# Spreading the k-tiles of the conditioning product over four column groups of TensorE

## The chip, the cores and the metric

The kernel runs on one core of a Trainium2 chip. The metric is the device time of one execution in microseconds, as the median over runs; smaller is better.

## The reference, cut to what matters

The reference chains two transformer blocks. The second one is modulated by a conditioning vector: for each of its two layers

```
adaln(cond, w, b) = silu(cond) @ w + b        # cond: 1024 values, w: 1024 x 6144
mod_lat = adaln(c,     mod_w[i], mod_b[i])
mod_ctx = adaln(c_ctx, mod_w[i], mod_b[i])
sh1, sc1, g1, sh2, sc2, g2 = split(mod, 6)    # shifts, scales and gates of the layer
```

Both conditioning vectors (`c` and `c_ctx`) go through the same weights, so this is a product of a 2 x 1024 matrix with a 1024 x 6144 matrix, once per layer of the second block. It depends on nothing that the first block computes. The first block has two layers; each has a delta-rule branch (a blockwise triangular inverse followed by a recurrence over four chunks of 64 tokens), a sparse attention branch, a memory branch and a feed-forward part.

## The kernel before, in words

All weights come as slabs of 128 x 1024 f32 (512 KB) through a ring of six slots that the DMA queue of SyncE fills in the order in which TensorE uses them. TensorE, VectorE and ScalarE each run one long hand-ordered program; they meet at semaphores. Seven of the eight PSUM banks are handed out in turn; the eighth, `mod_bank`, belongs to the modulation for the whole first block: its columns 256 to 511 take the running sum of one group of 256 modulation values as a row (one partition for each conditioning vector), its columns 0 to 191 collect the values once they are turned into columns (one value per partition).

The 6144 modulation columns of a layer are cut into 24 groups of 256 (`MOD_GROUPS`). A group needs two slabs, each with four k-tiles of 128 x 256, so eight k-tiles make the sum. Of the 24 groups of a layer, the first 12 (`MODS_ALONE`) are computed in full f32 between other products of the first block's layer with the same number, by `some_mods`, line L1705; the other 12 are computed with rounded operands beside the gate and branch weights, by `mixed_mod`, line L1693. The change is about the first 12 of each layer: 24 groups in all.

For each of these groups TensorE (a) turns the row of the group before with `turn_mods` (L1675: two transposes of a 2 x 128 piece; the groups of `mixed_mod` use L1677, two products of a 4 x 128 piece with `fold4`), having waited for `mods_row`, and (b) runs eight matmuls with `cond[:, j, :]` (128 x 2) as the stationary operand and the k-tile (128 x 256) as the moving one, all accumulating in partitions 0 and 1 of `mod_bank`. The profile shows each f32 matmul as two records, so eight k-tiles are 16 records. ScalarE then copies the row out (`mod_rows`, L2165) into `mrow`, which has two slots.

Where the 12 groups of a layer stand in TensorE's order:

- four in the stage that builds the decay matrices, one ahead of the `cum` product (L1768) of each quarter g of the heads; ScalarE takes `exp` of that product (L2266), VectorE then works on it (L2749 and the lines behind it) and on `kk`/`kq` (L1775)
- two in the stage that turns the start of the inverse (`x0`, L1785), ahead of g = 0 and g = 2; behind it comes the inverse itself, whose first products are L1797, and which VectorE feeds with the masks of L2777
- four in the recurrence, one in each chunk ch, between the `rope` products (L1842) and the point at which TensorE waits for VectorE's `vnew` (L2824, reported by the memset of L2826); behind this wait come the state update (L1878, read by VectorE in L2838) and the chunk's output (L1881); the next chunk begins with L1858 and L1867
- two behind the second batch of index scores (L1890), ahead of the memory branch. In between, the first batch of scores waits for `index_rope` (VectorE L2810), and the sums L567 wait for squares of ScalarE.

Of the kernel before, what the change touches and what calls it, by code (L numbers as in the profile page):

```python
# [12 lines left out]
ACT = mybir.ActivationFunctionType  # L13
ALU = mybir.AluOpType
AXX = mybir.AxisListType.X

P = 128
D = 1024
KT = D // P
# [17 lines left out]
RING = 6  # L37
BANKS = 8
# [16 lines left out]
MOD_COLS = 256  # L55
MOD_GROUPS = MODS // 2
MODS_ALONE = 12
MIXED = 36
mixed_at = lambda i: 3 * (i // 2) + i % 2
ROPE_AT = ((0, 1, 2), (3, 4, 5), (6, 7, 8), (9, 10))  # L60
# [29 lines left out]
def make_consts():  # L90
    i = np.arange(P)
    same = (i[:, None] // CHUNK) == (i[None, :] // CHUNK)
    c = {}
# [42 lines left out]
    c["expert"] = np.repeat(e[None].astype(np.float32), P, 0)  # L136
    c["expert_slab"] = np.repeat((EXPERT_SLABS * e[None]).astype(np.float32), P, 0)
    c["tie"] = np.repeat((NE - 1 - e[None]).astype(np.float32), P, 0)
    return c


# [1219 lines left out]
def program(nc, dram, known):  # L1361
# [3 lines left out]
    with ctx:  # L1365

        def sb(name, shape, dt=F32):
            return ctx.enter_context(nc.sbuf_tensor(name, shape, dt))
# [11 lines left out]
        rope = sb("rope", [P, 4, T])  # L1380
        small = sb("small", [P, 640])
        tick = sb("tick", [P, 8])
        mrow = sb("mrow", [4, 2, MOD_COLS])
        cond4 = sb("cond4", [P, KT, 4], F32R)
        fold4 = sb("fold4", [4, 2])
        eps = sb("eps", [P, 4])
        mods = sb("mods", [P, DEPTH, 48, 2])
        cond = sb("cond", [P, KT, 2])
        arena_at = nc.sbuf_base
        arena = sb("arena", [P, 33 * T + 28 * T + 8 * 2048 + 1536])  # L1390
        A = arena[:, 0:33 * T].rearrange("p (k t) -> p k t", t=T)
# [267 lines left out]
        def _(pe):  # L1659
# [8 lines left out]
            def turn_mods(n):  # L1668


                pe.wait_ge(*c.at("mods_row", n))
                for i in range(MOD_COLS // P):
                    at = 2 * (n * (MOD_COLS // P) + i)
                    if n % MOD_GROUPS < MODS_ALONE:
                        last = nc.tensor.transpose(mod_bank[:, at:at + 2], mrow[0:2, n % 2, i * P:(i + 1) * P], ident[0:2, 0:2])  # L1675
                    else:
                        last = mm(mod_bank[:, at:at + 2], mrow[0:4, n % 2, i * P:(i + 1) * P], fold4[:, :], start=True, stop=True)  # L1677
                return last
# [18 lines left out]
            def some_mods(l, count):  # L1697
                for n in range(l * MOD_GROUPS + mod_next[l], l * MOD_GROUPS + mod_next[l] + count):
                    if n:
                        turn_mods(n - 1)  # L1700
                    for j in range(KT):
                        g = mod_slab(n, j // 4)
                        if j % 4 == 0:
                            pe.wait_ge(c.sem(f"slab_loaded{g % RING}"), 16 * (g // RING + 1))
                        last = mm(mod_bank[0:2, MOD_COLS:2 * MOD_COLS], cond[:, j, :], ring[:, g % RING, (j % 4) * MOD_COLS:(j % 4 + 1) * MOD_COLS],  # L1705
                                  start=j == 0, stop=j == KT - 1)
                        if j % 4 == 3:
                            last.then_inc(c.sem(f"slab_done{g % RING}"), 1)
                mod_next[l] += count
# [436 lines left out]
        def _(act):  # L2146
# [7 lines left out]
            def mod_rows(count):  # L2154
                nonlocal mods_read
                for n in range(mods_read, mods_read + count):
                    i = n % MOD_GROUPS - MODS_ALONE
                    if i >= 0:
                        name = f"{'gates' if i < MIXED // 6 else 'branch'}{n // MOD_GROUPS}"
                        act.wait_ge(c.sem("split_used"), stream.split[name] + 6 * (i % (MIXED // 6)) + 6)  # L2160
                        af(mrow[:, n % 2, :], c.banks[BANKS - 1][0:4, MOD_COLS:2 * MOD_COLS], ACT.Copy).then_inc(*sc.count("mods_row", n))
                        continue
                    g = mod_slab(n, 1)
                    act.wait_ge(c.sem(f"slab_done{g % RING}"), g // RING + 1)
                    af(mrow[0:2, n % 2, :], c.banks[BANKS - 1][0:2, MOD_COLS:2 * MOD_COLS], ACT.Copy).then_inc(*sc.count("mods_row", n))  # L2165
                mods_read += count
            act.wait_ge(*c.at("x_loaded", "all"))
            act.wait_ge(*c.at("vec_loaded", "all"))
            for l in range(DEPTH):
# [74 lines left out]
                    silu_tiles(2, half)  # L2244
                sa_read(6, 9)
                if l == 0:
                    af(cond[:, :, :].rearrange("p k s -> p (k s)"), v["cond"], ACT.Silu).then_inc(*sc.count("cond_silu", "all"))
                af(A[:, 24:32, :], A[:, 24:32, :], ACT.Silu).then_inc(*sc.count("z_silu", l))
                sa_read(9, 12)
                af(beta.rearrange("p (a b) -> p a b", a=2), stok[:, :, 64:72], ACT.Sigmoid).then_inc(*sc.count("beta", l))  # L2250
# [340 lines left out]
        def _(dve):  # L2591
# [5 lines left out]
            tt, ts, stt, copy = nc.vector.tensor_tensor, nc.vector.tensor_scalar, nc.vector.scalar_tensor_tensor, nc.vector.tensor_copy  # L2597
            for b in range(BANKS):
                nc.vector.memset(c.banks[b][:, :], 0.0).then_inc(c.sem(f"bank_read{b}"), 1)
            nc.vector.memset(eps[:, 0:1], EPS).then_inc(*ve.count())  # L2600
            nc.vector.memset(eps[:, 2:3], EPS * EPS).then_inc(*ve.count())
            nc.vector.memset(eps[:, 1:2], 1.0).then_inc(*ve.count("eps", "all"))
# [46 lines left out]
            for l in range(DEPTH):  # L2649
# [35 lines left out]
                for q in range(3, DN + SA):  # L2685
# [28 lines left out]
                        decay_sums(l)  # L2714
                    if l == 0 and q == DN + 20:
                        dve.wait_ge(*c.at("cond_silu", "all"))
                        copy(cond4[:, :, 0:2], cond[:, :, :]).then_inc(*ve.count())
                        tt(fold4[:, :], k["ident"][0:4, 0:2], k["ident"][0:4, 2:4], ALU.add).then_inc(*ve.count())
                        dve.wait_ge(*ve.last())
                        tt(cond4[:, :, 2:4], cond[:, :, :], cond4[:, :, 0:2], ALU.subtract).then_inc(*ve.count("cond_split", "all"))  # L2720
                    if DN + 9 <= q < DN + 13:
                        unit_part(1, q - DN - 9)
                dve.wait_ge(*c.at("sums_exp", l))
# [788 lines left out]
```

## Time and profile before

| | |
|---|---|
| median of 3 runs | 3823.14 us (3821.86 to 3825.27) |
| span of the profiled execution | 3827.3 us |
| TensorE busy | 3643.8 us (95%) |
| VectorE busy | 2413.5 us (63%) |
| ScalarE busy | 1898.2 us (50%) |
| busy with L1705 | 89.7 us in 384 records |
| mean granted TensorE clock | 0.979 |

The profiled execution's own device time isn't given apart from its span; nothing but the span is known of it, and the span lies 4.2 us above the median of the runs. The records of a pipelined matmul overlap: one of L1705 lasts 0.38 us, but the next starts about 0.22 us later. So times of a stage are read from start to start.

### The profile page before, as it was taken

How to read it: one execution, taken by the hardware profiler on the slowest of the kernel's cores; microseconds unless marked ns; L12 is line 12 of the kernel's file. 1: busy time of each engine (PE TensorE's matmuls, PEld its weight loads, DVE VectorE, ACT ScalarE, POOL GpSimd, SP SyncE). 2: the span in 40 equal slices, each digit the busy share in tenths (PEclk: the TensorE clock that was granted, in tenths of full speed). 3: DMA queues.
4: the chain of work that ended last, by engine and by line, in shares of the span. 5: the costliest groups of instructions: out<-in, count | busy, mean ns of one | idle time of the engine just before them, and what ended most of it. 6: DMA issues, size and time to landing. Idle time of an engine off the chain costs nothing.

```text
span 3827.3 us, 63424 instructions
## 1 busy us (share of the span) xinstructions
PE 3643.8 (95%) x24076; PEld 3163.2 (83%) x24076; DVE 2413.5 (63%) x3717; ACT 1898.2 (50%) x2845; POOL 8.4 (0%) x16
## 2 busy tenths in 40 slices
PE   7999999999999999999998999998999999999998
PEld 7977899899997789999868999976787877776664
DVE  7555656756745665775657656545555555688887
ACT  6532465444643246454345434354444444577775
POOL 0000000000000000000000000000000000000000
PEclk9999999999999999999999999998999999999999
DMA  6441347565542336655312555530455555699996
GB/s 204 132 133 51 116 150 219 177 182 159 166 141 63 101 105 207 212 182 183 111 52 87 180 183 182 171 111 19 150 183 170 184 170 184 224 343 347 348 350 248
DMA packets 181900, 657.92 MB, mean 172 GB/s; under 512 B 20208, under 2 KB 22256, under 8 KB 181056
## 3 DMA queue, kind: packets, MB, share of 16 engines
q1 hardware_dynamic: 180576, 648.39, 52.0%
q0 software_dynamic: 1120, 6.67, 0.5%
q8 instruction: 146, 2.39, 0.3%
q14 instruction: 58, 0.48, 0.0%
HBM read 653.92 MB, written 1.05 MB: 171 GB/s over the span
## 4 chain that ended last, share of the span: by engine, by line
PE 86%; DVE 9%; ACT 3%; issue 2%; DMA 1%; SPq 0%; ACTq 0%; DVEq 0%; POOL 0%
PE bank L788 15%; PE bank L790 15%; PE bank L789 15%; PE bank L1161 6%; PE bank L1163 5%; PE bank L1162 5%; PE bank L1185 3%; PE bank L1187 3%; PE bank L1186 3%; PE bank L608 2%; PE bank L1705 1%; PE bank L1693 1%; PE bank L629 1%; PE bank L1797 1%; PE bank L388 1%
## 5 line engine op out<-in xcount | busy, mean ns | idle before, releaser
L1286 DVE TENSOR_TENSOR moe_w_low<-ring,moe_w_high 128x1024 fp32r<-128x1024 f32 x528 | 640.6, 1224 | 269.5 <-ACT moe_w_high L1226 261.1
L1226 ACT ACTIVATE moe_w_high<-ring 128x1024 fp32r<-128x1024 f32 x528 | 556.1, 1060 | 335.1 <-PE bank L1163 218.5
L827 DVE TENSOR_TENSOR gates_w_low<-ring,gates_w_high 128x1024 fp32r<-128x1024 f32 x292 | 354.3, 1223 | 206.2 <-ACT gates_w_high L812 205.8
L812 ACT ACTIVATE gates_w_high<-ring 128x1024 fp32r<-128x1024 f32 x292 | 306.0, 1055 | 233.2 <-PE bank L790 226.4
L1161 PE MATMUL bank<-moe_w_high,picked_high 128*128 128x512 f32 (+4 forms) x968 | 390.0, 403 | 17.7 <-DVE moe_w_low L1286 17.7
L1163 PE MATMUL bank<-moe_w_high,picked_low 128*128 128x512 f32 (+4 forms) x968 | 382.9, 396 | 0.0
L1162 PE MATMUL bank<-moe_w_low,picked_high 128*128 128x512 f32 (+4 forms) x968 | 382.2, 395 | 0.0
L827 DVE TENSOR_TENSOR ffn_w_low<-ring,ffn_w_high 128x1024 fp32r<-128x1024 f32 (+2 forms) x176 | 194.9, 1114 | 121.9 <-ACT ffn_w_high L812 121.7
L812 ACT ACTIVATE ffn_w_high<-ring 128x1024 fp32r<-128x1024 f32 (+2 forms) x176 | 170.1, 969 | 159.2 <-PE bank L790 159.2
L788 PE MATMUL bank<-first_x_high,first_w_high 128*128 128x256 f32 x848 | 246.5, 291 | 1.3 <-DVE first_w_low L827 1.1
L789 PE MATMUL bank<-first_x_high,first_w_low 128*128 128x256 f32 x848 | 243.7, 287 | 0.0
L790 PE MATMUL bank<-first_x_low,first_w_high 128*128 128x256 f32 x848 | 243.6, 287 | 0.0
L827 DVE TENSOR_TENSOR first_w_low<-ring,first_w_high 128x1024 fp32r<-128x1024 f32 x122 | 148.8, 1223 | 143.4 <-ACT first_w_high L812 142.4
L1161 PEld LDWEIGHTS bank<-moe_w_high,picked_high 128*128 128x128 f32 (+4 forms) x968 | 164.7, 170 | 78.7 <-DVE moe_w_low L1286 21.7
L1163 PEld LDWEIGHTS bank<-moe_w_high,picked_low 128*128 128x128 f32 (+4 forms) x968 | 164.8, 170 | 61.4
L1162 PEld LDWEIGHTS bank<-moe_w_low,picked_high 128*128 128x128 f32 (+4 forms) x968 | 165.0, 170 | 53.6
L1185 PE MATMUL bank<-moe_w_high,hid_high 128*128 128x512 f32 (+4 forms) x484 | 191.9, 396 | 10.7 <-DVE hid_low L1301 10.1
L788 PE MATMUL bank<-ffn_x_high,ffn_w_high 128*128 128x256 f32 x704 | 200.1, 284 | 1.0 <-DVE arena L3154 0.8
L789 PE MATMUL bank<-ffn_x_high,ffn_w_low 128*128 128x256 f32 x704 | 199.2, 283 | 0.0
L790 PE MATMUL bank<-ffn_x_low,ffn_w_high 128*128 128x256 f32 x704 | 199.2, 283 | 0.0
L1187 PE MATMUL bank<-moe_w_high,hid_low 128*128 128x512 f32 (+4 forms) x484 | 191.1, 395 | 0.0
L1186 PE MATMUL bank<-moe_w_low,hid_high 128*128 128x512 f32 (+4 forms) x484 | 190.9, 394 | 0.0
(547 smaller groups left out, 9658.2 us busy)
## 6 DMA issues: line engine op xcount, KB each, us to landing
ring<-in_moe SPq DMA_DIRECT2D x528, 512.0 KB, 4.9
ring<-in_w_in SPq DMA_DIRECT2D x138, 512.0 KB, 3.6
ring<-in_w_ffn SPq DMA_DIRECT2D x132, 512.0 KB, 3.6
ring<-in_even_ffn SPq DMA_DIRECT2D x132, 512.0 KB, 3.6
ring<-in_w_gates SPq DMA_DIRECT2D x72, 512.0 KB, 4.4
ring<-in_w_branch SPq DMA_DIRECT2D x72, 512.0 KB, 4.5
ring<-in_mod_w SPq DMA_DIRECT2D x48, 512.0 KB, 3.6
ring<-in_w_mem SPq DMA_DIRECT2D x32, 512.0 KB, 3.6
```

The lines of the kernel that those rows point to most:

```text
L788: nc.tensor.matmul(out, wh, xh, start=start, stop=False, skip_group_check=True)
L789: nc.tensor.matmul(out, wl, xh, start=False, stop=False, skip_group_check=True)
L790: last = nc.tensor.matmul(out, wh, xl, start=False, stop=stop, skip_group_check=True)
L812: nc.scalar.activation(high[:, s % 3, 0:width], ring[:, g % RING, 0:width], ACT.Copy).then_inc(c.sem("high_ready"), 1)
L827: subtract(low[:, s % 3, 0:width], ring[:, g % RING, 0:width], high[:, s % 3, 0:width], ALU.subtract)\
L1161: mm(out, xh, wh, start=i == 0, stop=False)
L1162: mm(out, xh, wl, start=False, stop=False)
L1163: last = mm(out, xl, wh, start=False, stop=i == KT - 1)
L1185: mm(out, hh, wh, start=n == 0 and f == 0, stop=False, skip_group_check=True)
L1187: last = mm(out, hl, wh, start=False, stop=n == MOE_CHUNKS - 1 and f == 1, skip_group_check=True)
L1226: nc.scalar.activation(high[:, (s0 + q) % 3, :], ring[:, (g0 + q) % RING, :], ACT.Copy).then_inc(c.sem("high_ready"), 1)
L1286: tt(low[:, (s0 + q) % 3, :], ring[:, (g0 + q) % RING, :], high[:, (s0 + q) % 3, :], ALU.subtract)\
```

## The change

`cond` gets 32 columns for each k-tile (`GROUP`), of which two hold the conditioning vectors and 30 are zero (cleared once at the start). The k-tile j goes to column group j mod 4: its result lands in partitions 32 (j mod 4) to 32 (j mod 4) + 31 of the bank, so the four k-tiles of one slab go to four different groups, and each group accumulates two k-tiles. The row copied by ScalarE has now 128 partitions instead of 2. The four partial sums are added by the product that turns the row: a matmul of the 128 x 128 piece with a constant 128 x 2 matrix `fold_groups` that has a one wherever the partition modulo 32 equals the column. The constant makes the table of constants two columns wider. The groups of `mixed_mod` are as before.

```
+GROUP = 32
+    c["fold_groups"] = (i[:, None] % GROUP == np.arange(2)[None, :]).astype(np.float32)
...
-        mrow = sb("mrow", [4, 2, MOD_COLS])
+        mrow = sb("mrow", [P, 2, MOD_COLS])
-        cond = sb("cond", [P, KT, 2])
+        cond = sb("cond", [P, KT, GROUP])
...
                     if n % MOD_GROUPS < MODS_ALONE:
-                        last = nc.tensor.transpose(mod_bank[:, at:at + 2], mrow[0:2, n % 2, i * P:(i + 1) * P], ident[0:2, 0:2])
+                        last = mm(mod_bank[:, at:at + 2], mrow[:, n % 2, i * P:(i + 1) * P], k["fold_groups"], start=True, stop=True)
...
-                        last = mm(mod_bank[0:2, MOD_COLS:2 * MOD_COLS], cond[:, j, :], ring[:, g % RING, (j % 4) * MOD_COLS:(j % 4 + 1) * MOD_COLS],
-                                  start=j == 0, stop=j == KT - 1)
+                        sums = mod_bank[GROUP * (j % 4):GROUP * (j % 4 + 1), MOD_COLS:2 * MOD_COLS]
+                        last = mm(sums, cond[:, j, :], ring[:, g % RING, (j % 4) * MOD_COLS:(j % 4 + 1) * MOD_COLS],
+                                  start=j < 4, stop=j >= 4)
...
-                        af(mrow[:, n % 2, :], c.banks[BANKS - 1][0:4, MOD_COLS:2 * MOD_COLS], ACT.Copy).then_inc(*sc.count("mods_row", n))
+                        af(mrow[0:4, n % 2, :], c.banks[BANKS - 1][0:4, MOD_COLS:2 * MOD_COLS], ACT.Copy).then_inc(*sc.count("mods_row", n))
...
-                    af(mrow[0:2, n % 2, :], c.banks[BANKS - 1][0:2, MOD_COLS:2 * MOD_COLS], ACT.Copy).then_inc(*sc.count("mods_row", n))
+                    af(mrow[:, n % 2, :], c.banks[BANKS - 1][:, MOD_COLS:2 * MOD_COLS], ACT.Copy).then_inc(*sc.count("mods_row", n))
...
-                    af(cond[:, :, :].rearrange("p k s -> p (k s)"), v["cond"], ACT.Silu).then_inc(*sc.count("cond_silu", "all"))
+                    act.wait_ge(*c.at("cond_cleared", "all"))
+                    af(cond[:, :, 0:2], v["cond"].rearrange("p (k s) -> p k s", s=2), ACT.Silu).then_inc(*sc.count("cond_silu", "all"))
...
+            nc.vector.memset(cond[:, :, :].rearrange("p k s -> p (k s)"), 0.0).then_inc(*ve.count("cond_cleared", "all"))
             nc.vector.memset(eps[:, 0:1], EPS).then_inc(*ve.count())
...
-                        copy(cond4[:, :, 0:2], cond[:, :, :]).then_inc(*ve.count())
+                        copy(cond4[:, :, 0:2], cond[:, :, 0:2]).then_inc(*ve.count())
...
-                        tt(cond4[:, :, 2:4], cond[:, :, :], cond4[:, :, 0:2], ALU.subtract).then_inc(*ve.count("cond_split", "all"))
+                        tt(cond4[:, :, 2:4], cond[:, :, 0:2], cond4[:, :, 0:2], ALU.subtract).then_inc(*ve.count("cond_split", "all"))
```

## Rows read from the trace of the kernel before

**Rows 1.** The page: busy time by engine; the chain that ended last.

```profile
PE 3643.8 (95%) x24076; PEld 3163.2 (83%) x24076; DVE 2413.5 (63%) x3717; ACT 1898.2 (50%) x2845; POOL 8.4 (0%) x16
...
PE bank L788 15%; PE bank L790 15%; PE bank L789 15%; PE bank L1161 6%; PE bank L1163 5%; PE bank L1162 5%; PE bank L1185 3%; PE bank L1187 3%; PE bank L1186 3%; PE bank L608 2%; PE bank L1705 1%; PE bank L1693 1%; PE bank L629 1%; PE bank L1797 1%; PE bank L388 1%
```

**Rows 2.** Groups by form, TensorE: L1705 (busy us, mean ns of one, idle before).

```profile
L1705 PE MATMUL bank<-ring,cond 128*2 128x256 f32 x384 | 89.7, 388 | 0.0
```

**Rows 3.** Timeline, program start (start, us, engine, line, form, count, idle before and releaser).

```profile
0.94 4.27 DVE L2599 MEMSET bank<- 128x512 f32 x8 [0.94 <-PEq L3507]
...
8.41 1.28 ACT L468 ACT_TABLE_LOAD   x1 [8.41 <-DMA vecs<-in_vecs]
```

**Rows 4.** Timeline, layer 0: first decay quarter, and start of the inverse.

```profile
236.48 0.35 DVE L2749 TENSOR_SCALAR arena<-bank,small 128x128 f32<-128x128 f32 x1 [0.86 <-ACT arena L2266]
...
270.16 2.50 DVE L2777 TENSOR_TENSOR squares<-arena,consts 128x512 f32<-128x512 f32 x4
...
270.91 3.84 PE L1797 MATMUL bank<-arena,squares 128*128 128x128 f32 x32
```

**Rows 5.** Timeline, layer 1: the same places, and the last L1705 between them.

```profile
1146.91 0.35 DVE L2749 TENSOR_SCALAR arena<-bank,small 128x128 f32<-128x128 f32 x1 [1.39 <-ACT arena L2266]
...
1176.04 6.55 PE L1705 MATMUL bank<-ring,cond 128*2 128x256 f32 x16
...
1180.59 2.50 DVE L2777 TENSOR_TENSOR squares<-arena,consts 128x512 f32<-128x512 f32 x4
...
1183.45 3.74 PE L1797 MATMUL bank<-arena,squares 128*128 128x128 f32 x32
```

**Rows 6.** Windows, layer 1: PE, PEld, DVE, ACT, POOL busy, PEclk, DMA, GB/s.

```profile
1175.60:1179.00 3.40, 3.26 (x10) 1.15 (x11) 3.36 (x8) 1.04 (x3) 0.00 (x0) 0.50 0.00 1
```

**Rows 7.** Timeline, layer 0, chunk 2 of the recurrence.

```profile
361.43 2.79 PE L1842 MATMUL bank<-arena,consts 128*128 128x512 f32 x6
...
363.47 1.28 DVE L2824 TENSOR_TENSOR arena<-arena,bank 64x512 f32<-64x512 f32 x2
364.15 0.28 PE L1675 MATMUL bank<-consts,mrow 2*128 2x2 f32 x2
364.36 3.62 PE L1705 MATMUL bank<-ring,cond 128*2 128x256 f32 x16
...
367.91 2.05 PE L1878 MATMUL bank<-arena 64*128 64x128 f32 x16
...
369.17 2.16 DVE L2838 SCALAR_TENSOR_TENSOR arena<-arena,small,bank 128x128 f32<-128x128 f32 x8 [4.30 <-PE bank L1878]
```

**Rows 8.** Timeline, layer 0, chunk 3 and what follows it.

```profile
378.83 0.06 DVE L2826 MEMSET tick<- 128x1 f32 x1
...
381.06 1.66 PE L1881 MATMUL bank<-arena 64*128 64x64 f32 x13
...
382.45 0.37 PE L1890 MATMUL bank<-arena 64*128 64x128 f32 x1
...
382.56 0.27 PE L1881 MATMUL bank<-arena 64*128 64x64 f32 x1
...
385.69 6.08 PE L567 MATMUL bank<-consts,squares 128*128 128x2 f32 x32 [0.66 <-ACT squares L2298]
```

**Rows 9.** Timeline: index scores alone, a turn by products, a 128-partition copy.

```profile
398.75 2.10 PE L1890 MATMUL bank<-arena 64*128 64x256 f32 x16
...
1141.01 0.60 PE L1677 MATMUL bank<-fold,mrow 4*128 4x2 f32 x4
...
1137.62 0.38 ACT L2232 ACTIVATE arena<-bank 128x256 f32<-128x256 f32 x1 [2.50 <-PE bank L790]
```

**Rows 10.** Timeline, layer 0: L1858 in chunks 1 and 2, and VectorE ahead of the memory branch.

```profile
342.14 3.47 PE L1858 MATMUL bank<-arena 128*64 128x128 f32 x16
...
357.73 1.93 PE L1858 MATMUL bank<-arena 128*64 128x128 f32 x16
...
405.53 0.48 DVE L2853 SCALAR_TENSOR_TENSOR arena<-arena,small,consts 128x256 f32<-128x256 f32 x1 [0.43 <-ACT arena L2310]
```

## The prediction, made blind

> **What bounds the kernel now.** I read the page first: TensorE is busy for 95% of the span and the chain that ended last is almost all TensorE, yet L1705 has only 1% of it [rows 1]. The reader is to see the size of the stake: the 24 groups hold TensorE for 89.7 us [rows 2], 2.3% of the span, and no version of the change can give back more. Next I read the timeline around each of the 24 places, because TensorE isn't last everywhere there. The places fall into four kinds, below. All times come from the profiled execution, whose span is 3827.3 us, 4.2 us above the median of the runs (3823.1 us); I work out a difference and take it off the median. A measurement of this kernel can tell 0.2%, 7.6 us, from no change.
>
> **The price of one group now.** In chunk 2 the turn starts at 364.15, the 16 records of L1705 at 364.36 and the next product at 367.91 [rows 7]: 0.21 us and 3.55 us, 3.76 us together. The 3.62 us of the 16 records less the last one's 0.38, over 15, give 0.216 us a record.
>
> **The price of one group after.** No column group other than one fixed group is in use in the trace next to another, so the price is bounded. The nearest rows are those of two *row* groups: L1890 has 64-row operands, alternately in partitions 0 to 63 and 64 to 127, and the same 256 columns in f32 as L1705. Its 16 records take 2.10 us [rows 9]: (2.10 - 0.37) / 15 = 0.115 us a record, half of 0.216. Two groups do run side by side, in f32. And they aren't held up by the order of the program: a record of L1890 starts at 382.45, ahead of one of L1881 at 382.56, which was issued before it and works on the other half of the rows [rows 8]. That matters, since the two records of one k-tile go to the same column group, one after the other in program order.
>
> - Lower end: each of four groups has 2 k-tiles x 2 records x 0.213 = 0.85 us, plus the 0.14 us that a group of 16 has today over 16 x 0.213 (3.55 - 3.41): 1.0 us.
> - Upper end: nothing overlaps and each change of column group lets the array run empty. A record then lasts its full 0.38 us once in each k-tile: 8 x (0.38 - 0.21) = 1.3 us on top of 3.55: 4.9 us.
> - I take 1.2 us, the lower end plus 0.2 us for four staggered starts and loads, because the L1890 rows show the ideal factor for their two groups.
>
> The Trainium skill, page "TensorE: Matmul & The Clock Gate", section "Part 3: Packing small matmuls", says that small matmuls in different row or column groups overlap, giving for three column groups 2.38 times the speed; but also that matmuls start and end strictly in program order. By that rule two neighbouring records of one group block the queue behind them; the rows of L1881 and L1890 speak against it. What it would do here is the first rival.
>
> **The turn** gets four records instead of two, with 128 x 128 pieces. L1677 has such a piece with 4 rows, in four records: it starts at 1141.01 [rows 9] and the L1705 behind it at 1141.54, so 0.53 us instead of 0.21: +0.32 us. (That more rows cost nothing is a choice: 64-row and 128-row records have the same pace in L1881 and L1867.) A group after: 1.2 + 0.53 = 1.73 us, a saving of S = 3.76 - 1.73 = 2.03 us where TensorE is last.
>
> **Recurrence, four places a layer.** In chunk 2 VectorE has its `vnew` at about 364.8 (363.47 + 1.28 and a memset) while TensorE comes to L1878 only at 367.91 [rows 7]: TensorE is last, with 3.1 us of slack behind it. The two move together from chunk to chunk: L1878 is followed by L2838 on VectorE after 1.26 us (369.17), and next to it stand VectorE's rope steps, so VectorE alone would need about 11 us a chunk against TensorE's 14. S = 2.03 is under 3.1, so chunks 0, 1 and 2 give S in full: 6 x 2.03 = 12.2 us in two layers. In chunk 3 VectorE reports at 378.83 but TensorE comes at 381.06 [rows 8]: 2.2 us, again more than S. But the scores behind (L1890) wait for VectorE's rope steps, finished at about 382.2; from there 1.1 us of L1890 and 0.9 us of transposes lead to L567 at about 384.4 to 385.0, where it starts at 385.69 now. ScalarE's squares, 2 us earlier, no longer hold it. I take 1.0 us a layer: 2.0 us.
>
> **Decay stage, four places a layer.** Here VectorE is last: it starts its first quarter at 236.48 and the masks of the inverse at 270.16 [rows 4], 33.7 us for four quarters, 8.4 us each, where TensorE has 6.6 us of work each. Three of the four groups are therefore hidden now and their saving is worth nothing. The first is not: VectorE is idle for 0.86 us before 236.48 for the `exp` that stands behind L1705 and L1768, and 1.39 us in layer 1 [rows 4, 5]. Both go: 2.25 us.
>
> **Start of the inverse, two places a layer.** In layer 0 the inverse's first product starts 0.75 us after the mask work (270.16, 270.91): hidden. In layer 1 the distance is 2.86 us, because L1705 took 6.55 us: granted clock 0.50, the 1.2 GHz level, after TensorE had been idle for about 3 us waiting for ScalarE's copy [rows 4 to 6]. The change gives 2.86 - 0.75 = 2.1 us back. But it also takes work from TensorE just where it idles most. Shorter groups in this stage leave about 4 us of idle in each 8.4 us, and the clock may go down in layer 0 too and stay down into L1797. What such a stretch costs is in the rows: L1858 took 3.47 us instead of 1.93 in chunk 1 [rows 10], 1.5 us. I charge one such stretch in each layer: -3.0 us, of 0 to -6.
>
> **Ahead of the memory branch, two places a layer.** TensorE is idle for 4 us behind them; VectorE and ScalarE are last. VectorE waits 0.43 us for ScalarE, which waited for L1705 [rows 10]: 0.9 us in two layers. The rest is hidden by VectorE's score work.
>
> **The rest.** The last turn of the 12 stands in the gate stage, where TensorE is last: 2 x 0.32 = -0.6 us. ScalarE's copy costs the same: 0.38 us for 128 x 256 [rows 9], as long as for 2 x 256. The memset of `cond` is half as wide as one of L2599, 4.27 / 8 / 2 = 0.27 us, and delays VectorE and ScalarE by nothing, since ScalarE waits until 8.41 us for its vectors [rows 3]; without that cover it costs 0.27 us. The new wait for `cond_cleared` is long met. The two columns of constants are 8 bytes in 12.6 KB. No DMA moves or waits: the slabs are asked for earlier by at most 2 us, at a third of the DMA's share.
>
> **Sum.** 12.2 + 2.0 + 2.25 + 2.1 - 3.0 + 0.9 - 0.6 = 15.9 us off 3823.1: 3807 us (span 3811).
>
> **The rivals.**
>
> - *Half the overlap (in order, or a shared read path).* If the second record of a k-tile must start before any record of the next k-tile, only neighbours overlap: 9 x 0.213 + 0.14 = 2.06 us a group, S = 3.76 - 2.59 = 1.17. Sum: 7.0 + 2.0 + 1.35 + 0.9 - 0.6 = 10.7 us: 3812 us. For it: the four k-tiles side by side are each 128 rows of moving data, where L1890's two row groups need 64 rows each. Against it: the overtaking record.
> - *No overlap at all.* The change doesn't do what it says; 3.55 us stay and 0.32 come on top at the 8 open places and the 2 last turns, with the small ends: +3 to +4 us, 3827 us.
> - *Slower: the array runs empty at each change of column group.* 4.9 us a group, +1.65 at the 8 open places, 13 us, with 2 us at the other places: 3838 us. It decides (over 7.6 us) once L1705 takes more than 4.0 us a group.
> - *The clock takes it back.* If TensorE, now less busy, is granted the low level in six or more further stretches at 1.5 us each, 9 us go: about 3816 us. For it: rows 5 and 6. Against: most of the 12 places a layer stand in dense work.
>
> Another page of the Trainium skill, "TensorEngine Tiling (Array Packing)", section "Key Properties", has a rule against the change, that a switch of tiling mode drains TensorE. The 0.14 us above are what a switch can cost today in L1705, which is already 2 columns wide; no row shows more.
>
> **Chances.** Full overlap 0.52, half 0.20, none 0.13, slower by draining 0.06, clock 0.09. Low end of the range: 1.0 us a group (+1.6), no clock loss (+3): 3802. High end: it takes in half overlap (3812) and the clock case (3816) with 4 us for further low stretches: 3820; no overlap and draining, 0.19, stay out. The likeliest case alone: 3802 to 3811. Faster by over 0.2% (under 3815.5): 0.52 + 0.17 from half overlap = 0.69. Within: 0.03 + 0.13 + 0.08 = 0.24. Slower: 0.07.
>
> **What would show it.** Right: L1705's 16 records in about 1.5 us from first start to last end, with starts of different k-tiles some 0.05 us apart; L1878 in chunk 2 about 1.7 us behind the start of the turn; no idle before L2749's first; L1797 in layer 1 under 1 us behind L2777. Wrong: 16 records over 2 us (the half case), over 3.5 us (none); TensorE idle ahead of L1878 for `vnew` (my slack is wrong); L1797 at twice its 3.7 us (clock).

## The result and the profile after

| | before | after |
|---|---|---|
| median | 3822.0 us (5 runs, 3820.1 to 3825.3) | 3795.2 us (5 runs, 3793.8 to 3814.0) |
| ratio of the two | | 0.9942, 95% interval 0.9927 to 0.9958 |
| span of the profiled execution | 3827.3 us | 3793.4 us |
| mean granted TensorE clock of it | 0.979 | 0.977 |

The kernel got faster by 22 us (16 to 28). That is the ratio of the means over the five runs each; the medians lie 27 us apart, because three of the five runs after were near 3794 us and the other two at 3805 and 3814 us. I had forecast 3807 us and a range from 3802 to 3820: the direction was right, the gain came out larger, and the median lies outside the range. Over everything that was run later, 17 runs of the kernel after have a mean of 3803.4 us (from 3793.8 to 3814.0) and 80 runs of the kernel before one of 3825.1 us: 21.7 us apart, with 3.9 us of uncertainty. So the gain stands; the 3795.2 us were among the lower of its runs, and the mean of all 17 lies inside the range.

The page of the kernel after, busy time by engine and the chain that ended last, to be held against [rows 1]:

```profile
PE 3583.1 (94%) x24124; PEld 3144.7 (83%) x24124; DVE 2413.3 (64%) x3718; ACT 1899.8 (50%) x2845; POOL 8.4 (0%) x16
...
PE bank L790 15%; PE bank L791 15%; PE bank L792 15%; PE bank L1163 6%; PE bank L1165 6%; PE bank L1164 6%; PE bank L1187 3%; PE bank L1188 3%; PE bank L1189 3%; PE bank L610 2%; PE bank L1695 1%; PE bank L631 1%; PE bank L1800 1%; PE bank L390 1%; DVE moe_w_low L1288 1%
```

TensorE's busy time fell by 60.7 us, and L1705, now L1708, is gone from the chain. The group by form shows that this is the product itself: as many records as in [rows 2], 29.1 us where there were 89.7 (busy us, mean ns of one, idle before). One record takes longer, 426 ns against 388; four run at a time.

```profile
L1708 PE MATMUL bank<-ring,cond 128*32 128x256 f32 x384 | 29.1, 426 | 0.0
```

Timeline of the kernel after, chunk 2 of layer 0, the place of [rows 7]:

```profile
346.30 3.46 PE L1861 MATMUL bank<-arena 128*64 128x128 f32 x16
...
353.34 0.06 DVE L2831 MEMSET tick<- 128x1 f32 x1
...
354.16 0.50 PE L1677 MATMUL bank<-consts,mrow 128*128 128x2 f32 x4
354.59 1.07 PE L1708 MATMUL bank<-ring,cond 128*32 128x256 f32 x16
355.59 2.05 PE L1881 MATMUL bank<-arena 64*128 64x128 f32 x16
```

From the start of the turn to the next product it is now 355.59 - 354.16 = 1.43 us, 0.43 for the turn and 1.00 for the group, instead of 3.76. The reader is to see two more things: `vnew` (the memset, 353.34) is still ready before TensorE asks for it at 355.59, and L1861 took 3.46 us here, at the low clock, where L1858 took 1.93 in [rows 10].

Timeline of the kernel after, layer 0, the second group at the start of the inverse and the inverse's first products ([rows 4]):

```profile
258.86 1.02 PE L1677 MATMUL bank<-consts,mrow 128*128 128x2 f32 x4 [5.76 <-ACT mrow L2168]
259.81 1.93 PE L1708 MATMUL bank<-ring,cond 128*32 128x256 f32 x16
...
263.71 2.50 DVE L2782 TENSOR_TENSOR squares<-arena,consts 128x512 f32<-128x512 f32 x4
...
264.64 5.10 PE L1800 MATMUL bank<-arena,squares 128*128 128x128 f32 x32
```

TensorE waits 5.76 us for ScalarE's copy, the group behind it runs at the low clock (1.93 us; the granted clock is 0.50 from 257.3 to 267.5), and so do the first products of the inverse: 5.10 us instead of 3.84.

**Where the 22 us lie.** One profile of each kernel isn't enough for that, as the experiments showed, so the table has two of the kernel before and three of the kernel after. Every number is a distance between two starts in a timeline; the stages are cut at VectorE's first step with KB (L2733, L2738 after), its first mask step (L2777, L2782), TensorE's L1858 (L1861) of chunk 0, the first weight load of L567 (L569; up to 0.2 us ahead of its first matmul), and VectorE's first MAX8 of the selection behind the scores.

| us, layer 0 / layer 1 | before | before again | after | after again | after, third |
|---|---|---|---|---|---|
| decay stage | 41.9 / 42.5 | 41.9 / 42.5 | 41.1 / 41.1 | 41.0 / 41.1 | 41.1 / 41.1 |
| inverse | 58.0 / 60.0 | 59.8 / 58.0 | 59.4 / 58.0 | 60.0 / 59.8 | 59.7 / 59.7 |
| four chunks | 57.6 / 55.9 | 55.9 / 57.5 | 49.4 / 50.3 | 50.1 / 50.2 | 50.4 / 50.5 |
| L567 to selection | 29.4 / 27.7 | 29.4 / 29.4 | 25.8 / 25.9 | 26.2 / 26.0 | 25.8 / 25.8 |
| these stages together | 372.9 | 374.3 | 351.0 | 354.4 | 354.1 |
| all the rest | 3454.3 | 3451.6 | 3442.4 | 3451.1 | 3446.3 |

The changed stages went from 373.6 to 353.2 us on average: 20.4 us. The rest of the program, in which nothing was changed, comes out anywhere within 12 us in these five profiles.

### The profile page after: what moved, and what is told of

The parts are those of the page before. It is cut to its first block, busy times and chain, and to the rows that moved or that the text cites. A ratio compares the mean times of both kernels' runs of the same rounds, so it can differ in the third digit from the quotient of the medians.

```text
span 3793.4 us, 63521 instructions
## 1 busy us (share of the span) xinstructions
PE 3583.1 (94%) x24124; PEld 3144.7 (83%) x24124; DVE 2413.3 (64%) x3718; ACT 1899.8 (50%) x2845; POOL 8.4 (0%) x16
## 4 chain that ended last, share of the span: by engine, by line
PE 85%; DVE 9%; ACT 3%; issue 2%; DMA 1%; DVEq 0%; ACTq 0%; SPq 0%; POOL 0%
PE bank L790 15%; PE bank L791 15%; PE bank L792 15%; PE bank L1163 6%; PE bank L1165 6%; PE bank L1164 6%; PE bank L1187 3%; PE bank L1188 3%; PE bank L1189 3%; PE bank L610 2%; PE bank L1695 1%; PE bank L631 1%; PE bank L1800 1%; PE bank L390 1%; DVE moe_w_low L1288 1%
```

## The experiments

They ran in four series, each kernel timed in five rounds beside the kernel before; a ratio is against the runs of before in the same series. Theory A: a group costs what one column group has to work through, and the gain is that saving where TensorE is last. Theory B: part of it, or of a loss, comes with the column groups themselves or with the clock. Others are named where they come up.

**1. The kernel after again**, no edit.

> The changed kernel once more, against the kernel before on the same chip. Theory A (the groups shrink from 3.76 to 1.43 us and the eight places where TensorE is last give nearly all of it): about 22 us faster, as in the first comparison (ratio 0.994), with L1708's group again 1.00 us from its first start to the next product. Theory B (part of the first gain was a clock that happened to be higher in that run, 5.6 us of it before the first changed instruction): nearer to the forecast 16 us, ratio 0.996, with single runs spread over 10 us and more.

Measured: 3802.4 us, ratio 0.9941 (0.9924 to 0.9958). The same gain, another median; the six runs spread over 18 us.

**2. All k-tiles in one column group**, the wide operand, the wide row and the new turn kept:

```
-    sums = mod_bank[GROUP * (j % 4):GROUP * (j % 4 + 1), MOD_COLS:2 * MOD_COLS]
+    sums = mod_bank[0:GROUP, MOD_COLS:2 * MOD_COLS]
-              start=j < 4, stop=j >= 4)
+              start=j == 0, stop=j == KT - 1)
```

> All eight k-tiles go to column group 0, with the 32-column stationary operand, the 128-row turn and the 128-partition copy kept: everything of the change but the spreading. Theory A (the overlap of the four groups is the whole gain): the 16 records take 3.6 us again, the turn costs 0.2 to 0.3 us more than the transposes, so 3 to 4 us slower than the kernel before (ratio 1.001). Rival (the wider operand or the product that turns the row is itself what helps, or the clock gains from it): clearly faster than before, by 5 us or more.

Measured: 3822.8 us, ratio 0.9995 (0.9985 to 1.0005). Timeline of this kernel, a group in the recurrence:

```profile
360.33 0.50 PE L1677 MATMUL bank<-consts,mrow 128*128 128x2 f32 x4
360.76 3.64 PE L1708 MATMUL bank<-ring,cond 128*32 128x256 f32 x16
364.33 1.94 PE L1881 MATMUL bank<-arena 64*128 64x128 f32 x15
```

The group takes 3.57 us, as before (3.55). Without the spreading no gain can be measured, and the 3 to 4 us that I had expected the padding and the longer turn to cost don't show either. One thing in its profile bears on the sum, though: its changed stages took 369.1 us, 4.5 us less than before on average, and the difference is in the last stage, 26.5 us in each layer instead of 29.0. There L567 ran at the high clock in both layers, without any spreading (us, PE busy, PEclk, DMA share, GB/s; layer 0):

```profile
382.23:385.96 3.73, 3.73 (x33) 1.00 0.02 4
```

From this kernel to the kernel after, which differ in nothing but the spreading, the changed stages go from 369.1 to 353.2 us, 15.9 us by one profile of it, and the means of all runs from 3822.3 to 3803.4 us, 18.9 us.

**3. Two column groups** (`j % 2`), and **4. four groups with the two k-tiles of a group next to each other in the program** (`j // 2` instead of `j % 4`, `start` and `stop` to match). The second asks about order: if records had to start in the order of the program, neighbours that go to one column group would block the others.

> The k-tiles alternate between column groups 0 and 1. Theory A (each group works through its own records at 0.213 us, whatever the others do): 8 records per group, 1.7 us plus 0.14, so 1.85 us a group in place of 1.00; the gain is 3.76 - 2.28 = 1.5 us at the open places, about 13 us in all. Rival (the groups aren't independent; a fixed cost, not the number of groups, sets the 1.00 us): the group stays near 1.0 us or near 2.1 us or more.

> Four column groups, but k-tiles 2i and 2i+1 go to the same group i, so that its four records stand next to each other in program order. Theory A (a record waits only for its own column group; TensorE takes a later one ahead of it, as L1890 ahead of L1881 in the rows of before): still about 1.0 us a group and the same time as the changed kernel. Rival (records start strictly in program order, as the first rival of the prediction has it): the blocks of four only overlap at their seams, 13 x 0.213 + 0.14 = 2.9 us a group, and the kernel is 14 us slower than the changed one, some 8 us faster than before.

Measured: two groups 3808.6 us, ratio 0.9947 (0.9934 to 0.996); neighbours 3805.7 us, 0.9957 (0.9944 to 0.997). Timelines, first two groups, then neighbours:

```profile
345.99 1.92 PE L1708 MATMUL bank<-ring,cond 128*32 128x256 f32 x16
347.84 1.82 PE L1881 MATMUL bank<-arena 64*128 64x128 f32 x14
```

```profile
347.71 1.09 PE L1708 MATMUL bank<-ring,cond 128*32 128x256 f32 x16
348.73 1.49 PE L1881 MATMUL bank<-arena 64*128 64x128 f32 x11
```

1.85 us for eight records in each of two groups, 1.02 us for four in each of four, whatever the order of the program. The starts in the trace show how: in both kernels with four groups the 16 records start in four bursts of four, some 0.22 us apart. The four of a burst start within 0.02 us in the kernel after and within 0.04 us in neighbours, where the first four of the program all go to one column group; so records of the other groups start ahead of some of these. Every price fits 0.213 us x the records of one column group + 0.15: 3.56, 1.85 and 1.00. The rival "half the overlap" is refuted as a price (2.06 us), and so is draining at a change of group. By their totals, though, two and four groups can't be told apart (I had expected 13 us for two, and the total gave 20); the timelines can, and so can the changed stages, 360.2 us with two groups (13.4 less than before) and 351.7 in neighbours.

**5. The kernel before with two of its eight k-tiles.** It leaves six of the eight k-tiles out of each modulation sum and uses no column groups:

```
+    if j % 4 < 3:
+        continue
-              start=j == 0, stop=j == KT - 1)
+              start=j == 3, stop=j == KT - 1)
```

> The kernel before, with six of the eight k-tiles of each of the 24 groups left out of the modulation sum (their slabs are still loaded and released, the rows are still copied and turned by transposes). TensorE then issues four records a group, as many as each column group gets in the kernel after, and no operand is wider than two columns. Theory A (the gain is nothing but the shorter group, whatever shortens it): a group takes 0.85 to 1.0 us and the turn 0.21, so this is at or a little under the kernel after, 0.992 to 0.995 of before. Theory B (part of the gain or of the loss comes with the column groups themselves, 128 busy columns that change the clock or the reads): the ratio differs from that of the kernel after (0.9942) by more than 0.002, and its changed stages, 354 us in the repetition of the kernel after, come out more than 5 us away from that.

Measured: 3810.8 us, ratio 0.9966 (0.9953 to 0.9979). Timeline:

```profile
345.08 0.28 PE L1675 MATMUL bank<-consts,mrow 2*128 2x2 f32 x2
345.30 1.02 PE L1707 MATMUL bank<-ring,cond 128*2 128x256 f32 x4
346.25 2.05 PE L1880 MATMUL bank<-arena 64*128 64x128 f32 x16
```

Four records alone take 0.95 us, sixteen over four groups 1.00: the overlap is complete to 0.05 us. The ratio came out above the 0.992 to 0.995 of theory A and 0.0024 above that of the kernel after, the first of the two things that theory B had asked for, though the intervals overlap; the second failed, the changed stages took 353.9 us, like those of the kernel after. The excess is in the unchanged stages (3456.2 us), which can't tell the reason. In layer 0 L567 took 6.83 us here; that comes back below.

**6. Only the four groups of the recurrence spread**, and **7. only the eight others**. In both, `SPREAD` lists the groups of a layer that are spread; the others go to one column group and are turned from two rows:

```
+    wide = n % MOD_GROUPS in SPREAD        # 6: (6, 7, 8, 9)   7: the eight others
+    at = GROUP * (j % 4) if wide else 0
```

> The kernel after, but only the four groups in the recurrence of each layer are spread; the eight others put all k-tiles into column group 0 (3.57 us) and their row is turned from two partitions. Theory A (the recurrence pays in full, 7 of 8 places at 2.3 us, and the rest is small): 16 to 18 us, 0.9955. Theory C (the decay stage and the inverse pay as much as the recurrence, since they lost 6 us in layer 0 and 3.4 in layer 1 in the profiles): 10 to 12 us, 0.997. By the prediction on record it would be 14 of the 16 us.

> The complement: the eight groups of each layer outside of the recurrence are spread, the four inside are not. Theory A: the first decay wait (1 to 1.4 us a layer) and 1 to 2 us at the inverse less what the low clock takes: 2 to 5 us, 0.999. Theory C: 8 to 12 us, 0.9975. Theory D (where TensorE idles more it is granted less, and the clock takes back what these groups give): 0 us or slower, at most 1.0.

Measured: recurrence alone 3810.1 us, ratio 0.996 (0.9945 to 0.9974); elsewhere alone 3818.6 us, 0.9987 (0.9978 to 0.9996). 15 us and 5 us, together 20: they add up to the whole, the ratio of the recurrence a little short of the 16 to 18 us of theory A. Three quarters of the gain are in the recurrence. Elsewhere, the groups that VectorE hides gave neither 8 to 12 us (theory C) nor nothing (theory D). The changed stages of their profiles, 353.6 and 366.0 us against 369.1 with one column group, have the same order: 15.5 and 3.1 us, though together 2.7 more than the 15.9 between one column group and four.

**8. The groups of the recurrence moved into the decay stage**, two behind `kk` and `kq` of each quarter, none in the chunks. TensorE idles 4 to 6 us in some quarters there.

```
     (kk, kq of quarter g)
+    some_mods(l, 2)                        # instead of 1 ahead of cum
...
-    some_mods(l, 1)                        # chunk ch
```

> The kernel after with the four groups of the recurrence moved into the decay stage: two groups behind kk and kq of each quarter instead of one ahead of cum, none in the chunks. TensorE idles 4 to 6 us of each 8.4 us there and a pair takes 2.9 us, so they should be hidden, and each of three chunks a layer gives back 1.43 us: 8 to 11 us more than the kernel after, ratio about 0.9915. If the recurrence has no slack left for it (VectorE's vnew comes last: 0.3 to 1.5 us of slack are left by the profile of after), only 3 to 5 us: 0.993. If the pair holds up ScalarE's exp or the cum product of the next quarter, or the clock falls in the recurrence, nothing: 0.994 to 0.996.

Measured: 3807.4 us, ratio 0.996 (0.9945 to 0.9975): no gain on the kernel after. The chunks did give 6.9 us, 46.1 and 47.3 us instead of 50.2 each, short of the 8.6 expected; `vnew` now comes last (in layer 0 TensorE waits for it 0.72, 0.67 and 1.60 us in chunks 1 to 3); but the inverse stage went from 59.4 to 62.1 and 62.4. Timeline, end of the decay stage of layer 0:

```profile
262.34 1.02 PE L1677 MATMUL bank<-consts,mrow 128*128 128x2 f32 x4 [0.48 <-ACT mrow L2167]
...
263.29 1.94 PE L1708 MATMUL bank<-ring,cond 128*32 128x256 f32 x16
...
264.59 2.50 DVE L2780 TENSOR_TENSOR squares<-arena,consts 128x512 f32<-128x512 f32 x4
...
267.65 1.07 PE L1708 MATMUL bank<-ring,cond 128*32 128x256 f32 x16
...
269.58 3.74 PE L1800 MATMUL bank<-arena,squares 128*128 128x128 f32 x32
```

Both groups of the pair behind the last quarter wait for ScalarE's copy (2.56 us and 0.48), the granted clock is 0.50 from 260.7 to 267.5, and the pair and the group behind it stand ahead of the inverse: it starts 5.0 us after the first mask step (269.58 - 264.59) instead of 0.9. The changed stages together took 353.3 us, no less than in the kernel after.

**9. The same without that pair** (one more behind quarters 0, 1 and 2; the group of chunk 3 stays), with **10. the five hidden groups kept long** (`SPREAD = (0, 6, 7, 8, 9, 10, 11)`), and **11. the kernel after a third time**.

> The kernel after with three of the four groups of the recurrence moved: one more behind kk and kq of the decay quarters 0, 1 and 2, none behind quarter 3, whose pair held up the start of the inverse by 3 to 4 us in the kernel moved; the group of chunk 3 stays. If that pair was the reason: the inverse stage stays at 59 to 61 us, the recurrence comes to 42 to 43 us, changed stages 347 to 349 us, ratio 0.992 to 0.994. If the extra turns hold up the cum product of the last quarter instead, the decay stages grow by as much as the recurrence gives, and the sum stays at 352 to 354 us.

> The kernel after, but the five groups of each layer that VectorE hides (three in the decay stage, two at the start of the inverse) are left in one column group at 3.57 us, so that TensorE doesn't idle there; the other seven are spread. Theory D (shorter groups there only make TensorE idle, and the low clock that follows costs 1.4 to 2 us at the inverse of layer 0 and 0 to 2 in layer 1, and more behind it): no low clock between the first decay quarter and the inverse, the inverse stage at 59.2 us in both layers, changed stages at 350 to 352 us, 2 to 3 us under the kernel after. Theory A without the clock: at most as fast as the kernel after.

> The kernel after again, for how far runs of one program differ. Theory A (the changed stages give 19 to 22 us, and the unchanged ones come out up to 6 us apart from execution to execution for the low clock alone): ratio 0.994 to 0.996, changed stages 351 to 355 us by the profile, unchanged ones anywhere from 3442 to 3456 us. Theory E (the change itself also speeds up the unchanged stages): the unchanged stages again lie below 3451 us, the sum that they have in the profile of the repetition, while those of the kernel before lie at 3454.

Measured: moved early 3800.3 us, 0.9933 (0.992 to 0.9946); kept busy 3808.9 us, 0.996 (0.9946 to 0.9975); after a third time 3807.0 us, 0.9951 (0.9932 to 0.997).

In moved early the pair was the reason: the inverse is back at 59.6 us. The chunks, at 48.9 and 45.8 us, missed the expected 42 to 43, which was set too low, since three times 1.43 us off 50.2 are 45.9; and in layer 0 a low stretch lies on the end of chunk 1 and the start of chunk 2. The sum of the changed stages is 356.4 us and no better than that of the kernel after, because L567 to selection went from 25.9 to 29.8 and 29.6. Timeline and window (us, PE busy, PEclk, DMA share, GB/s) of L569 in layer 0:

```profile
376.65 6.82 PE L569 MATMUL bank<-consts,squares 128*128 128x2 f32 x32
```

```profile
376.65:383.47 6.82, 6.82 (x34) 0.50 0.01 2
```

Theory D fell with kept busy: its inverse stages took 60.6 and 59.0 us, where it had asked for 59.2 in both, and its changed stages 353.6 us, where it had asked for 350 to 352. The low clock still came, only into the long group (6.54 us instead of 3.64) ahead of the inverse, as it did in layer 1 of [rows 5]. Where the low stretch falls on the group it delays the inverse, where it falls behind it the inverse itself runs slowly: both cost 1 to 2.6 us over the 58.0 us of an inverse stage without one. The third run of the kernel after came out within what theory A allows, with changed stages of 354.1 us and 3446.3 us for the rest; that is also below 3451 us, as theory E has it, so the kernel before had to decide.

**12. The kernel before again**, no edit.

> The kernel before, unchanged, as its own control and for a second profile of it. Theory A: ratio 1.000 within 0.002; the changed stages again at 370 to 373 us against 351 to 354 us in three profiles of the kernel after, so that 17 to 21 us lie there; the unchanged stages anywhere from 3442 to 3457 us. Theory E (the unchanged stages are slower in the kernel before): they again lie at 3454 us or above.

Measured: 3828.2 us, ratio 1.0006 (0.9997 to 1.0016), changed stages 374.3 us, the rest 3451.6 us. Theory A held but for 1.3 us in the changed stages, which it had at 373 us at most. Theory E had asked for 3454 us or more in the rest and isn't borne out: 3451.1 us were also measured in the kernel after.

**The low clock behind the chunks.** With two profiles of before the change in the last stage could be read. The window of the 32 records of L567, first before, then before again (layer 0):

```profile
385.69:391.77 6.08, 6.08 (x33) 0.58 0.01 3
```

```profile
381.91:387.71 5.80, 5.80 (x33) 0.62 0.01 3
```

and the same records in the kernel after and in its repetition:

```profile
372.54:376.27 3.73, 3.73 (x33) 1.00 0.02 4
```

```profile
379.48:383.36 3.88, 3.88 (x34) 0.94 0.01 4
```

In both layers of both profiles of before L567 takes 5.57 to 6.08 us, in the six layers of the three profiles of after 3.72 to 3.88. That is 2.1 us a layer, for a product that the change doesn't touch. Where the low stretch went can be seen in the repetition of the kernel after; the end of chunk 3 in its timeline, and the windows of chunk 3:

```profile
365.48 1.93 PE L1861 MATMUL bank<-arena 128*64 128x128 f32 x16
...
372.72 2.00 PE L1884 MATMUL bank<-arena 64*128 64x64 f32 x16 [0.26 <-DVE tick L2831]
...
376.01 1.77 PE L1893 MATMUL bank<-arena 64*128 64x128 f32 x16 [1.30 <-DVE arena L2815]
...
377.72 1.97 PE L1902 MATMUL bank<-consts,arena 128*128 128x128 f32 x8
...
379.48 3.88 PE L569 MATMUL bank<-consts,squares 128*128 128x2 f32 x32
```

```profile
365.48:372.50 7.02, 6.98 (x58) 1.00 0.05 20
372.50:376.00 3.50, 2.00 (x16) 1.00 0.77 295
376.00:379.48 3.48, 3.46 (x24) 0.58 0.01 5
```

TensorE waits for `vnew` (0.26 us) and then 1.30 us for VectorE's rope steps; behind that wait L1893 and L1902 run at a clock of 0.58 (L1902 1.97 us, where the kernel before has 1.09), and L567 is back at the high one.

## Why the prediction was right in direction and too small

Set against its own sum, with the averages of the table, over both layers:

| term of the sum | forecast | measured |
|---|---|---|
| decay stage, the wait for `exp` | 2.25 | 2.3 |
| inverse, 2.1 back less 3.0 for the clock | -0.9 | -1.0 |
| four chunks, 12.2 + 2.0 | 14.2 | 13.1 |
| L567 to selection | 0.9 | 6.1 |
| sum | 16.4 | 20.4 |

The last turn in the gate stage (forecast -0.6) can't be told from the scatter there.

- **The step that failed is the clock.** The prediction let the clock only take, 3.0 us, and only at the inverse. It had L567 at 6.08 us among its rows [rows 8] and used it as a fixed length, though the same 32 records run in 3.73 us at the high clock: 2 x 2.1 = 4.2 us of the 5.2 us that the last stage gave over the forecast. It isn't the shorter group that brings it: the kernel with all k-tiles in one column group also has L567 at 3.73 us in both layers, and moved early, with short groups, has it at 6.82. Nor is it the draw of single executions alone: L567 takes 5.57 us or more in all four layers of before, and 3.72 to 3.88 us in all 16 layers of the eight profiles that turn the row by products, use one or four column groups and leave the groups in their places (4.33 and 4.35 us with two column groups). What puts the low stretch on it or off it was not isolated; the longer turn and the wider operand, which all eight share, stand as a rival to small shifts of the work ahead of it.
- **Against one column group the sum was nearly right.** From that kernel to the kernel after, the decay stage gave 2.3 us, the inverse -1.9, the chunks 14.4 and the last stage 1.1: 15.9 us together, where the forecast has 16.4. This rests on one profile of that kernel, and the agreement of the total is in part luck, since the term of the inverse is off by 1 us. It leaves 4.5 of the 20.4 us to what the change does besides spreading, or to the draw of the clock, and the forecast had nothing for either.
- **The other 1.0 us of the last stage** can be of the same kind: L581 took 5.26 us on average in the four layers of before (4.33 to 5.73), and 4.59 us in the six layers of after (4.35 to 5.07), 1.3 us less over two layers. The 0.43 us that VectorE waited ahead of L2853 [rows 10] are gone, as forecast.
- **The price of a group** was set too high: 1.00 us, the lower end, not 1.2. The 0.2 us that I had added for staggered starts aren't there: the four groups start within 0.02 us, where I had looked for 0.05 between two k-tiles. And the turn takes 0.43 us in the recurrence instead of 0.53; its first weight load starts there under the product ahead of it, at 353.73 in the kernel after, 0.43 us before its first matmul. S is 3.76 - 1.43 = 2.33 us, not 2.03, and the distance from chunk to chunk shows it. Timeline, start of each chunk in layer 0 and the product behind the last one, first the repetition of before, then that of after:

```profile
326.01 1.96 PE L1858 MATMUL bank<-arena 128*64 128x128 f32 x16
...
340.01 1.93 PE L1858 MATMUL bank<-arena 128*64 128x128 f32 x16
...
353.99 1.93 PE L1858 MATMUL bank<-arena 128*64 128x128 f32 x16
...
367.96 1.93 PE L1858 MATMUL bank<-arena 128*64 128x128 f32 x16
...
381.91 5.80 PE L567 MATMUL bank<-consts,squares 128*128 128x2 f32 x32 [0.66 <-ACT squares L2298]
```

```profile
329.17 1.96 PE L1861 MATMUL bank<-arena 128*64 128x128 f32 x16
...
340.76 1.93 PE L1861 MATMUL bank<-arena 128*64 128x128 f32 x16
...
352.31 3.31 PE L1861 MATMUL bank<-arena 128*64 128x128 f32 x16
```

The third chunk starts 27.98 us behind the first before, 23.14 after: 2.4 us less for each of two chunks.
- **The chunks still gave less than forecast**, 13.1 for 14.2 us, because the clock took it back in two places of each layer. In chunk 2 the low stretch lies on L1861 in all six layers (3.31 to 3.60 us instead of 1.93), so that chunk gives 0.8 us instead of 2.4; in the kernel before a chunk is struck like that in one layer of two, as in [rows 10]. And chunk 3, forecast at 1.0 us, gave nothing: 14.00 us (365.48 to 379.48) against 13.95 (367.96 to 381.91), and 14.1 to 14.2 us in four of the other five layers of after. Only layer 0 of the first profile of after has 13.15: there the low stretch lies on L1861 at the start of the chunk, and not behind the wait. I had counted VectorE's rope steps as the next thing in line, correctly, but not what a TensorE that waits for them is granted afterwards.
- **The decay stage** was right to 0.1 us. VectorE's 33.7 us are unchanged in all five profiles; only the wait ahead of them went.
- **The inverse** was right to 0.1 us as a sum, for a mixed reason: both layers of before have 58.0 us in one profile and about 59.9 in the other, so the 2.1 us that I read in layer 1 as the state before were the draw of one execution. In the second profile of before, the long group stands in layer 0. Timeline:

```profile
261.70 6.31 PE L1705 MATMUL bank<-ring,cond 128*2 128x256 f32 x16
```

- **The range** allowed for unknown costs and not for how far runs lie apart. 17 runs of the kernel after go from 3793.8 to 3814.0 us, and its three medians are 3795.2, 3802.4 and 3807.0 us. Two of the three lie inside the range; that the first one doesn't is in part the draw of five runs, and that the others do is no proof of the sum, which was 4 to 6 us short.

What stays open: why the unchanged stages differ by up to 16 us over all profiles (3439.8 us in the kernel moved, 3456.2 us in the one with two k-tiles), and whether they differ by kernel. Low stretches move from one execution to the next from the first 230 us on, ahead of the first of the 24 groups (start to L2733 228.2 and 224.3 us in the two profiles of before), so an edit isn't needed for it. But the kernel with two k-tiles ran eight times within 3803.6 to 3814.0 us at the same changed stages as the kernel after, and I can't say that this is chance.

## What to carry to other kernels

A product with a stationary operand of few columns that accumulates over many k-tiles can be spread over four column groups at no cost in width, and the fold can ride on a product that turns the result anyway; the saving counts only where TensorE comes last, here at six of 24 places (chunks 0 to 2 of each layer, in chunk 2 with most of it lost to the low clock again) and in part at the first group of each layer. Work that is taken from an engine just where it already waits can move the low-clock stretches, and so, it seems, can smaller edits; what they moved here was as much as the smaller terms of the sum: look up, for each product near the change, at which of its two speeds it runs in the profile before, and treat a slow one as something that can be gained as well as lost. Two profiles of the kernel before would have shown which of its stretches are stable.

## What the runs showed of the hardware

- In f32, matmuls into four different column groups overlap almost completely: 16 records in 1.00 us, four alone in 0.95, eight in each of two groups in 1.85, all sixteen in one group in 3.57.
- They overtake each other: with the two k-tiles of one group next to each other in the program it is 1.02 us, and the first four starts lie within 0.04 us, though the first four records of the program share a group. The Trainium skill, page "TensorE: Matmul & The Clock Gate", section "Part 3: Packing small matmuls", has matmuls start and end strictly in program order; the starts and the price in these runs don't agree with that, and the measurement decides here.
- Moving all groups from 2 columns into a fixed group of 32 columns, and from 2-row transposes to 128-row products, changed nothing measurable in the total: 0.9995 (0.9985 to 1.0005), so at most 5.7 us.
- The same 32 records of L567 took from 3.71 (moved) to 6.83 us (two k-tiles), at a granted clock of 1.00 to 0.50, the 2.4 and the 1.2 GHz level. The form of the product doesn't set the level; behind a wait of TensorE of 1.30 us the clock was 0.58 for the next 3.5 us, behind the same wait (1.17 us) in moved early it stayed low through L569.
